# Layer 1 prompt attention: compressed-branch units dealt among the next head's wide units, banks split three and three

## The reference, cut to what matters

```python
lc = einsum('bqgrd,bcgd->bqgrc', qi, kcmp) * scale      # compressed blocks: 31 keys for the prompt
pc = masked_softmax(lc, cmp_end <= q_pos);  o_cmp = pc @ vcmp
ls = qi . k_sel * scale;  o_sel = masked_softmax(ls) @ v_sel   # selected blocks
lw = qi . kw * scale;     o_win = masked_softmax(lw) @ vw      # sliding window of 512
o = g0 * o_cmp + g1 * o_sel + g2 * o_win                       # per-head sigmoid gates
```

## Time and profile before

| | us |
|---|---|
| median of 3 runs | 2348.34 (2336.81 to 2349.63) |
| the profiled execution | 2347.75 |
| its span, first to last instruction | 2346.1 |
| the stage's first score matmul starts at | 1172.2 |
| the stage's last copy ends at | 1390.2 |
| PE busy, share of the span | 2055.0, 88% |
| DVE, ACT, POOL busy | 1356.7, 789.6, 268.6 |

### The profile page before, as it was taken

How to read it: one execution, slowest core, us unless ns; L and a number is a source line. 1 busy time by engine, 2 the same in 40 slices (tenths; PEclk the granted TensorE clock), 3 DMA queues, 4 the chain that set the end, 5 groups by cost and what they waited for, 6 DMA issues and landing times. The chain is left out here.

```text
span 2346.1 us, 47705 instructions
## 1 busy us (share of the span) xinstructions
PE 2055.0 (88%) x18117; PEld 1863.6 (79%) x18117; DVE 1356.7 (58%) x2553; ACT 789.6 (34%) x1415; POOL 268.6 (11%) x430
## 2 busy tenths in 40 slices
PE   5986898879999996997699969988987687999998
PEld 3973765659999996995499969988965486999998
DVE  5336332458887634337366558777753358888732
ACT  3111331135544102013266654444521215454300
POOL 0002443000000000000012222212223100000000
PEclk8996898879999997997799989999997998999999
DMA  9348899353343221216410013434359513334321
GB/s 372 100 160 334 280 342 366 118 192 90 91 109 104 81 69 49 82 55 252 156 47 2 2 56 121 122 94 127 109 186 328 216 57 89 106 93 109 99 75 63
DMA packets 238678, 322.56 MB, mean 137 GB/s; under 512 B 18424, under 2 KB 195013, under 8 KB 231148
## 3 DMA queue, kind: packets, MB, share of 16 engines
q1 hardware_dynamic: 215317, 239.18, 31.4%
q0 software_dynamic: 21248, 77.62, 9.5%
q10 hardware_dynamic: 1887, 2.73, 0.3%
HBM read 311.56 MB, written 16.42 MB: 140 GB/s over the span
## 5 line engine op out<-in xcount | busy, mean ns | idle before, releaser
L2637 PE MATMUL ps<-CHi,W1H 128*128 128x256 f32 x768 | 222.2, 289 | 36.9 <-DVE CLo L2740 36.9
L2638 PE MATMUL ps<-CLo,W1H 128*128 128x256 f32 x768 | 220.3, 287 | 0.0
L2639 PE MATMUL ps<-CHi,W1L 128*128 128x256 f32 x768 | 220.1, 287 | 0.0
L957 PE MATMUL ps<-XHup,WLup 128*128 128x272 f32 x640 | 185.1, 289 | 0.0
L957 PE MATMUL ps<-XHup,WHup 128*128 128x272 f32 x640 | 183.8, 287 | 1.3 <-DVE G L1106 1.3
L957 PE MATMUL ps<-XLup,WHup 128*128 128x272 f32 x640 | 184.5, 288 | 0.0
L2637 PEld LDWEIGHTS ps<-CHi,W1H 128*128 128x128 f32 x768 | 150.5, 196 | 38.8 <-DVE CLo L2740 28.2
L2158 DVE TENSOR_REDUCE NM<-ps 128x1 f32<-128x128 f32 (+1 forms) x224 | 89.5, 402 | 124.7 <-PE ps L2037 88.4
L484 PE MATMUL ps<-XHdn,WHdn 128*128 128x272 f32 x704 | 148.3, 292 | 12.1 <-DMA Wmod<-in_w_mod 5.2
L2117 ACT ACTIVATE P<-ps,NM 128x128 f32<-128x128 f32 (+1 forms) x224 | 101.3, 458 | 160.8 <-DVE NM L2158 155.9
L2638 PEld LDWEIGHTS ps<-CLo,W1H 128*128 128x128 f32 x768 | 150.7, 196 | 0.0
(11 more groups left out here) (564 smaller groups left out, 5338.4 us busy)
## 6 DMA issues: line engine op xcount, KB each, us to landing
H<-in_w_up SPq DMA_DIRECT2D x72, 512.0 KB, 5.1
Wearly<-in_w_mod SPq DMA_DIRECT2D x24, 1024.0 KB, 11.9
RAWdn<-in_w_down SPq DMA_DIRECT2D x14, 1408.0 KB, 6.4
RINGf<-in_cache_fox_k SPq DMA_DIRECT2D x48, 256.0 KB, 6.3
RINGf<-in_cache_fox_v SPq DMA_DIRECT2D x44, 256.0 KB, 8.2
RINGf<-in_cache_fox_v POOLq DMA_DIRECT2D x44, 256.0 KB, 6.2
RAWin<-in_nsa_w_in SPq DMA_DIRECT2D x20, 512.0 KB, 3.6
RINGf<-in_cache_fox_k POOLq DMA_DIRECT2D x38, 256.0 KB, 5.8
```

Source lines behind the costliest of these rows:

```text
L957: last = self.nc.tensor.matmul(self.ps[:, bank + b, 0:HALF], wt[:, w, k, :], x[:, k, :], start=start and k == 0 and n == 0, stop=k == 3 an ...
L2637: nc.tensor.matmul(out, WH[:, sig, k, w], hi, start=(k == 0 and m == 0), stop=False, skip_group_check=True)
L2638: nc.tensor.matmul(out, WH[:, sig, k, w], lo, start=False, stop=False, skip_group_check=True)
L2639: last = nc.tensor.matmul(out, WL[:, sig, k, w], hi, start=False, stop=(k == KU - 1), skip_group_check=True)
```

## The change

It reorders the units. The wide groups of a head and the compressed group of the head before are now dealt as A0 A1 C0 A2 A3 C1 B0 B1 C2 B2 B3 C3, where C belongs to the head before. The first head has its eight wide units alone, and the last four units of the stage are the C of head 15. Groups are numbered in the order in which they are opened: A, B of a head, then C of the head before. The banks are 3 for scores, 2 for transposed units and 3 for results, so that group g has result bank g % 3 and its first value product waits for group g - 3 to be combined. The distances TURN, COPY, PV, LAG and COMBINE stay. Layer 0 passes no order and keeps its own.

```diff
-        S_BANKS, T_BANKS, O_BANKS, COMBINE = (2, 1, 1, 4) if beside else (4, 2, 2, 6)
+        S_BANKS, T_BANKS, O_BANKS, COMBINE = (2, 1, 1, 4) if beside else (3, 2, 3, 6)
-        units = [(g, i) for g in range(len(groups)) for i in range(PT_TILES)]
+        units = units or [(g, i) for g in range(len(groups)) for i in range(PT_TILES)]
...
-                            groups.append(dict(head=len(heads), keyset=base + 3 * e + n, ...
+                            (dense if n < 2 else compressed).append(dict(head=len(heads), keyset=base + 3 * e + n, ...
...
+            groups, units = [], []
+            for h in range(len(heads) + 1):
+                wide = [(len(groups) + n, i) for n in range(2) for i in range(PT_TILES)] if h < len(heads) else []
+                groups += dense[2 * h:2 * h + 2]
+                thin = [(len(groups), i) for i in range(PT_TILES)] if h else []
+                groups += compressed[h - 1:h] if h else []
+                for i in range(PT_TILES):
+                    units += wide[2 * i:2 * i + 2] + thin[i:i + 1]
+            self.prompt_attention(T, sems, groups, heads, keysets, [H[:, c, 0:TP] for c in range(8)], setup, store, units=units)
```

More of the change, by code:

```diff
@@ L1953, in prompt_tiles, with prompt_attention @@
         return T, {n: sem("pa_" + n) for n in names}
-    def prompt_attention(self, T, sems, groups, heads, keysets, outs, setup_dve, store, beside=None, values_act=None):
+    def prompt_attention(self, T, sems, groups, heads, keysets, outs, setup_dve, store, beside=None, values_act=None, units=None):
         nc, ps = self.nc, self.ps
         QS, P3, PTB, NM, RC, O, T2, ID, MASK, KT, PC = (T[n] for n in ("QS", "P3", "PTB", "NM", "RC", "O", "T", "ID", "MASK", "KT", "PC"))
-        S_BANKS, T_BANKS, O_BANKS, COMBINE = (2, 1, 1, 4) if beside else (4, 2, 2, 6)
+        S_BANKS, T_BANKS, O_BANKS, COMBINE = (2, 1, 1, 4) if beside else (3, 2, 3, 6)
         T_BANK, O_BANK = S_BANKS, S_BANKS + T_BANKS
         TURN, COPY, PV, LAG = 2, 3, 4, 9
-        units = [(g, i) for g in range(len(groups)) for i in range(PT_TILES)]
+        units = units or [(g, i) for g in range(len(groups)) for i in range(PT_TILES)]
         items, waiting = [], []
@@ L2488, in setup @@
                 nc.vector.tensor_copy(CM[:, :, 0:NCMP_P], self.cmask)
-            heads, keysets, groups = [], [], []
+            heads, keysets, dense, compressed = [], [], [], []
             for gp in range(2):
@@ L2502, in nsa_prompt @@
                             value = (lambda j, v=4 * n + g: VE[:, j, v, :]) if n < 2 else (lambda j, g=g: VE_C[:, g, :])
-                            groups.append(dict(head=len(heads), keyset=base + 3 * e + n, n_keys=TP if n < 2 else NCMP_P, chunk=gp * 4 + r, e=e,
+                            (dense if n < 2 else compressed).append(dict(head=len(heads), keyset=base + 3 * e + n, n_keys=TP if n < 2 else NCMP_P, chunk=gp * 4 + r, e=e,
                                                first=n == 0, closes=e == 1 and n == 2, gate=GT[:, :, head * NSA_BR + branch], bias=None, mask=CM,
@@ L2506, in nsa_prompt @@
                         heads.append(dict(src=PT[own, gp * 4 + r, 0:TP], own=own, other=other))
-            self.prompt_attention(T, sems, groups, heads, keysets, [H[:, c, 0:TP] for c in range(8)], setup, store)
+            groups, units = [], []
[7 more added lines that the diff above has]
+            self.prompt_attention(T, sems, groups, heads, keysets, [H[:, c, 0:TP] for c in range(8)], setup, store, units=units)
     def key_pages(self, engine, b, half, dst, full):
```

## The result

The changed kernel takes 2372.31 us (median of 4, 2369.57 to 2374.52), the kernel before in the same runs 2346.51 (2336.81 to 2349.63). The ratio is 1.0117 with a 95% interval of 1.0092 to 1.0142: slower by 26 us, where +9.4 (2357) with a range up to 2367 was forecast. The profiled execution took 2371.16, its span 2369.5.

A forecast was written before the change was run, and what follows sets the result against it. TensorE, busy 88% of the span, was taken to bound the kernel. Profiled 2347.75 + 8.8 (regular stalls) + 0.6 (end), with keys and score banks at 0, gave 2357 us, 0.4% slower; 8-in-10 range 2345 to 2367.

The forecast's parts named there:

- the named wait: TensorE's value product of C (line 2075) waits for DVE's combine (line 2178), 14 times, about 0.9 us.
- The regular term: Blocks 2 to 15: 14 x (0.92 + 0.18 - 0.47), new stalls less the old wait, +8.8 us.
- the chain: DVE's sequence from A3's maximum through the combines of B and C, seen by TensorE at 3.03 us against its 2.11.
- Three score banks at nothing: Scores wait for the exponential of s - 3, already waited for or covered by ACT's copy: no cost.
- The term that decides, 0.92 a block: C's first value product waits for its only result bank, behind two combines in a row: 0.92 us, 14 times.
- t = 0: Start of the stall sum: the moment TensorE ends the scores of A3, step 4 of a block.
- The second small stall, 0.18: B3's transpose, step 0 of the next block, waits for C2's transpose bank: 1.86 against 1.68, 0.18 us.
- The old wait, taken off at 0.47: Once a head in the old order, TensorE waits for an exponential before a transpose; mean 0.47 us, expected to go.
- Middle keys 0, within 3: Second key/value pair's keys, made in heads 7 to 10, cost the same as before: 0, 3 us either side.
- The rival of keys or clock: Key sets add to the combine's stall (2363), or the clock falls for a quarter of the stage (2367); chance 0.06.
- Head 1's keys 0, within 1: Head 1's keys and queries are asked for a few steps earlier: 0, 1 us to either side.
- End +0.6: Last out item: three combines in a row on DVE where two stood, part of one 0.96 showing, +0.6 us.

The follow-up runs named there:

- e1: Kernel before, old unit order, with the new banks (3 for scores, 2 for transposed units, 3 for results): 2342.5 us, ratio 0.9991.
- e9: Changed kernel, but POOL adds branch B only once DVE has combined C as well: 2370.0 us, ratio 1.0113.
- e10: Changed kernel with the second pair of key/value heads using the first's keys, none made in the middle (output not the reference's): 2363.1 us, ratio 1.0087.
- e11: Kernel before with the second pair of key/value heads using the first's keys (output not the reference's): 2339.7 us, ratio 0.9984.
- e16: Kernel before, old order, with DVE's combine cut in three and begun one step earlier (step + 5 and + 6): 2337.9 us, ratio 0.9965.
- e12: Changed kernel with the first six key sets made at the steps of the order before (0, 0, 2, 6, 10, 14): 2368.5 us, ratio 1.0089.
- e2: Changed kernel with banks 2 for scores, 2 for transposed units, 4 for results: 2370.9 us, ratio 1.0102.

## Why the prediction was wrong

The sign, the place and the named wait were right; the size was not: +26 us where +9.4 was forecast, above the range. Two steps failed. The regular term, 14 x 0.63 = 8.8, measures 18.0; half of the 9.2 between them is that the chain left out how POOL's addition holds DVE's gate multiplication (14 x 0.33 = 4.6). And the terms put at 0, the keys and with them the clock, measure 13.5 in the profiled execution, with up to 8.1 by the lower granted clock in the middle. By the prediction's own steps:

- **Three score banks at nothing**: right in the old order (e1, 0.00 a pair), and in the new one no wait at line 2032 is in the rows of 1190 to 1400.
- **The term that decides, 0.92 a block**: right in kind and to 0.02 us along the chain down to C's reciprocal (forecast 1.94 after t = 0, measured 1215.34 - 1213.42 = 1.92). Mis-sized at the end: step 6 takes 2.26 where 1.00 was the work, 1.26. Of the 0.34 too little, 0.33 is POOL's addition beside the gate multiplication (e9). The rows held it: the view of that line has the multiplication at up to 0.38 before, and I priced it by the middle.
- **The second small stall, 0.18**: 0.17 in every other block and 0.36 in the rest (steps of 1.17 and 1.36 against 1.00). The sum left out that an out item shifts the steps, so that the combine of A (reciprocal at 1221.46) then stands before the maximum of B3:

```profile
1222.07 0.42 DVE L2178 TENSOR_TENSOR O<-ps,RC 128x256 f32<-128x256 f32 x1
...
1222.41 0.78 DVE L2158 TENSOR_REDUCE NM<-ps 128x1 f32<-128x512 f32 x2
...
1223.13 0.86 ACT L2117 ACTIVATE P<-ps,NM 128x512 f32<-128x512 f32 x2 [0.83 <-DVE NM L2158]
...
1223.87 0.42 PEld L2058 LDWEIGHTS ps<-CN,P 128*128 128x128 f32 x4 [0.56 <-ACT P L2117]
```

- **14 x 0.63 = 8.8**: 14 x 1.29 = 18.0 (e10 less e11). The old wait, taken off at 0.47, is nearer 0.38: so much longer is a block of before (12.93) than one of e16 (12.55), where no such wait is left. Some 0.1 of the 1.29 I can't lay to a step.
- **Middle keys 0, within 3**: 7.4 in the profile (25.3 in blocks 2 to 15 less 18.0). The stalls themselves came out as forecast, about the size of before (3.6 at the upper clock against 4.3). What failed is the clock, taken to stay up because it had after one gap of 1.04 us: it fell twice, for 20.5 us. The rival of keys or clock, given 0.06, came in together with the forecast and not in its place. Its price was misread too: 20% is the ratio at a mean clock of 0.84, a mixture of the two levels, and steps wholly at the lower level took 1.60 where 0.86 stood.
- **Head 1's keys 0, within 1**: 6.1 (first eight units 5.0, block 1 1.1). e12, by the steps of the first keys alone, has the first eight units back at 9.4. The stage starts at the lower clock; with the wide set at step 2 it stayed there until 1183.98, 18.8 us into the stage, and in e12 for 5.6 us. Other traces with the wide set at step 2 lose from 1.4 (e9) on.
- **End +0.6**: +1.1. Two gate multiplications of 0.60 beside POOL stand in it, where before had one of 0.38.

The rule weighed in the prediction (the Trainium skill, Perfetto Trace Analysis, Optimization Strategy, on repeated gaps and missing PSUM) would have been wrong for the old gap: e1 gives it a third result bank and the pair stays to 0.01 us. It fits the new one: with a fourth result bank (e2) the wait is gone, though the pair, at 27.81, is still not the old one.

The regular term as measured would have put the time at some 2366 (2347.75 + 18.0 + 0.6), still inside the range. What took it outside are the keys and the clock, bounded at 3 and 1 us. Why the clock falls under the new order and mostly not under the old is not shown; that the regular waits have a part in it is likely, since one fall came behind such a wait alone.

## What to carry to other kernels

With as many groups open as there are result banks, each kind of group has one bank: count the steps from a group's combine to the next use of that same bank. An in-order engine that waits for itself inside a chain of small instructions is held for the whole chain; putting the next unit's work between the links gave more here (25.10 us a pair where 25.86 stood, 7 us of the stage) than any reordering of units. Where a change adds waits to a busy TensorE, price the lower granted clock as a case of its own, by steps that ran wholly at that level, and look at the first units of a stage separately. One profile shows one draw of it: compare several traces before you name its size.

## What the runs showed of the hardware that I had not expected

- A DVE multiplication of two 4-column SBUF operands takes 0.17 us alone and 0.50 to 0.60 when it meets POOL's addition of 128 x 256 in SBUF; it then ends 0.02 us after the addition, at all 16 such places in the trace of the changed kernel. Moved apart in time it is 0.17 again (e9). The last multiplication of a combine, which reads PSUM, took 0.42 in all the rows above, and 0.42 at the one place in e9 where it overlaps with the addition (1407.51).
- The granted clock stayed at its upper level through one wait of 1.1 us every 14 us from 1190 to 1262, then fell for 3.4 us behind one more such wait, with no key set near; it fell again, for 17.1 us, behind waits of 1.07 and 0.82 within 2 us. In e10, with the same regular waits, it stayed up from 1175 to the stage's last units. The stage starts at the lower level, and in the changed kernel the ninth unit, 14 us of interrupted work later, still ran at it. What it needs to fall or rise these runs don't tell.
- A step of pure TensorE work that takes 0.86 us at the upper level took 1.60 at the lower one.
